# A decoder trunk: up- and query projections that begin with four units per input chunk instead of two, and a down unit whose weight halves are made in the last up pair

## The chip, the cores and the metric

The kernel runs on one core of a Trainium2 chip. The core has TensorE (PE, matrix products into PSUM), VectorE (DVE), ScalarE (ACT), GpSimd (POOL) and SyncE (SP, which issues the DMAs here). The metric is the time of one execution on the device in microseconds; lower is better. The engines run their own instruction lists in order and meet through semaphores.

## The reference

Two layers work on x (512 positions, 1024 features, float32). Each has a token mixer and a gated MLP, each inside a pre- and a post-norm, with a residual.

```python
for i in range(DEPTH):                       # DEPTH = 2
    hn = rmsnorm(x, norm_mix_pre[i])
    m = mamba2_mixer(hn, ...) if i % 2 == 0 else diff_attention(hn, ...)
    x = x + rmsnorm(m, norm_mix_post[i])
    hn = rmsnorm(x, norm_ffn_pre[i])
    f = conv_ffn(hn, ffn_w_up[i], ffn_conv_w[i], ffn_conv_b[i], ffn_w_down[i])
    x = x + rmsnorm(f, norm_ffn_post[i])
```

`conv_ffn` projects 1024 features to 2 x 2816, convolves causally with width 3, and projects silu(gate) * up back to 1024. `diff_attention` projects to q, k and v for 8 heads and subtracts one softmax from another.

## The kernel before, in words

Everything is kept transposed: 128 features on the partitions, 512 positions along the row. x is 8 chunks of 128x512.

*Units.* Each projection is a phase (MIX, SOUT, UP0, DN0, QKV, AOUT, UP1, DN1), and a phase is a row of units. A unit of an in-phase is one 128-column block of the weights, 128x1024, for one output tile of 128x512. To keep float32 accuracy each operand is split in two halves of the fast format: w = w_hi + w_lo, hn = hn_hi + hn_lo. `product` makes three matmuls for one chunk, (w_hi, hn_hi), (w_hi, hn_lo), (w_lo, hn_hi) (L354 to L356); a unit of 8 chunks is 24 matmuls. A down unit is half a contraction, 11 chunks, 33 matmuls.

*Weights.* SyncE loads unit j into `raw` (2 slots, `load_unit`, L310), once the low half of unit j-2 is made. `split_hi` (ScalarE, L317) copies it to w_hi, once unit j-2 has been multiplied, since w_hi and w_lo have two slots too. Then VectorE (`split_lo_dve`, L330), or GpSimd during the QKV phase (`split_lo`, L323), subtracts: w_lo = raw - w_hi. `ahead` lets a phase's loop make the halves of the next phase's first units.

*Banks.* A unit sums into one of two PSUM banks (`acc_of`); `wait_bank` holds TensorE until the tile two units back has been taken. b_x and b_y (two banks each) serve the state-space mixer, the start of SOUT and the attention scores.

*A boundary.* Between an out-phase and the next in-phase stand a post-norm, the residual and a pre-norm (`boundary_pe`, `boundary_act`, `boundary_dve`, `boundary_pool`). TensorE sums the squares over partitions (`sum_stat`, L449 and L453), ScalarE takes the root (L376), VectorE puts the inverse on a diagonal (L381), TensorE broadcasts it (`norm_bcast`, L409) into b_norm. Then, chunk by chunk: VectorE scales mbuf (L544), VectorE or GpSimd adds it to x (L560, L521), ScalarE makes hn_hi (L510) and the square (L425), VectorE makes hn_lo (L534), GpSimd adds up the squares (L441). TensorE multiplies each chunk by two units as it comes. The pre-norm's factor is not in hn: it is a factor of each position, so the projections start without it, and it is broadcast last and copied to r_pre (L516). Each output tile is multiplied by r_pre when VectorE takes it out of its bank (L706 in the MLPs, L1335 and L1338 for q, k and v). Boundary 1 leads from SOUT to UP0, 2 from DN0 to QKV, 3 from AOUT to UP1; 0 and 4 are the ends.

*MLP.* `ffn_dve` goes over 22 pairs (gate tile, up tile): take the gate tile, its convolution (L709, L715), take the up tile, its convolution, product with the Silu (L1150). In the middle of each convolution (`mid`) it makes the low half of a coming unit.

*Attention.* Round h projects q, k, v of head h (units 3h to 3h+2), while head h-1 is scored and head h-2 is finished. Round 0 has projections alone. TensorE writes scores to b_x and b_y; VectorE adds the bias (L1347) and takes the maximum (L1351), ScalarE the exponentials (L1278), VectorE combines the two softmaxes; TensorE transposes the weights of the four query blocks (t0 to t3, L1209) into b_cb, and ScalarE copies each out (L1286) before the next.

## Time and profile before

| | |
|---|---|
| median of 3 runs | 1544.0 us (1543.45 to 1544.49) |
| profiled execution: its own time, its span | 1545.04 us, 1542.9 us |
| busy, share of the span: TensorE | 1466.8 us, 95% |
| VectorE | 1019.0 us, 66% |
| ScalarE | 613.6 us, 40% |
| GpSimd | 212.2 us, 14% |
| mean granted TensorE clock | 0.980 |
| DMA | 142.04 MB, mean 92 GB/s |

The span runs from the first to the last instruction of the profiled execution. Busy time counts work and not waiting. The granted clock is the share of TensorE's full speed.

### The profile page before, as it was taken

To read this page: it belongs to the slowest core of one execution; us is meant where nothing else is said; L and a number is where in the kernel's file an instruction comes from. 1 tells how busy PE (TensorE), PEld (TensorE's weight loads), DVE (VectorE), ACT (ScalarE), POOL (GpSimd) and SP (SyncE) were. 2 spreads that over 40 slices of the span, in tenths; PEclk is the share of its full clock that TensorE was granted. 3 is DMA by queue.
4 is the path that set the end of the run, shared out by engine and by line. 5 is a ranking of instruction groups with operands and counts; after the bars stand their busy time and mean duration, and the time that the engine had idled before them with its cause. 6 is when DMAs were issued, how large, how long until landed. Compare 5 with 4: busy or idle time off the path is not lost.

```text
span 1542.9 us, 20707 instructions
## 1 busy us (share of the span) xinstructions
PE 1466.8 (95%) x6774; PEld 1161.7 (75%) x6774; DVE 1019.0 (66%) x1417; ACT 613.6 (40%) x953; POOL 212.2 (14%) x134
## 2 busy tenths in 40 slices
PE   6999999999997999999999799999888999999996
PEld 5778888888785888888888477776657888888885
DVE  6788888888328887778322657778258777775223
ACT  5655555556324222223222436556343222222221
POOL 3011101011213000000011432321140000000111
PEclk9999999999998999999999899999889999999998
DMA  4433333332220322223222121211112222223221
GB/s 148 154 123 123 135 121 110 136 122 82 83 94 31 106 90 89 93 95 111 94 93 83 36 88 55 68 54 55 48 62 72 92 95 95 95 95 113 94 93 55
DMA packets 36273, 142.04 MB, mean 92 GB/s; under 512 B 4048, under 2 KB 4176, under 8 KB 34192
## 3 DMA queue, kind: packets, MB, share of 16 engines
q1 hardware_dynamic: 36240, 141.62, 26.9%
q8 instruction: 18, 0.29, 0.1%
q14 instruction: 15, 0.12, 0.0%
HBM read 139.38 MB, written 2.23 MB: 92 GB/s over the span
## 4 chain that ended last, share of the span: by engine, by line
PE 74%; issue 10%; DVE 10%; POOL 3%; ACT 2%; DMA 1%; DVEq 0%; SPq 0%; POOLq 0%; ACTq 0%
PE bank L354 23%; PE bank L356 22%; PE bank L355 22%; POOL w_lo L323 3%; DVE hn_lo L534 2%; DVE w_lo L330 2%; DVE mbuf L544 1%; DMA raw<-w_mix 1%; DVE x L560 1%; DVE cv_s L715 1%; ACT w_hi L317 1%; PE b_y L731 1%; PE b_x L743 1%; PE b_y L734 1%; PE b_norm L453 0%
## 5 line engine op out<-in xcount | busy, mean ns | idle before, releaser
L354 PE MATMUL bank<-hn_hi,w_hi 128*128 128x512 f32 x1288 | 522.3, 406 | 43.1 <-DVE hn_lo L534 35.0
L355 PE MATMUL bank<-hn_lo,w_hi 128*128 128x512 f32 x1288 | 513.3, 399 | 0.0
L356 PE MATMUL bank<-hn_hi,w_lo 128*128 128x512 f32 x1288 | 513.1, 398 | 0.0
L317 ACT ACTIVATE w_hi<-raw 128x1024 fp32r<-128x1024 f32 (+1 forms) x217 | 239.7, 1104 | 499.9 <-PE bank L356 482.1
L330 DVE TENSOR_TENSOR w_lo<-raw,w_hi 128x1024 fp32r<-128x1024 f32 (+1 forms) x194 | 257.9, 1330 | 259.1 <-ACT w_hi L317 258.4
L354 PEld LDWEIGHTS bank<-hn_hi,w_hi 128*128 128x128 f32 x1288 | 244.7, 190 | 119.5 <-issue 30.0
L356 PEld LDWEIGHTS bank<-hn_hi,w_lo 128*128 128x128 f32 x1288 | 244.5, 190 | 59.6
L355 PEld LDWEIGHTS bank<-hn_lo,w_hi 128*128 128x128 f32 x1288 | 244.9, 190 | 55.6
L356 PE MATMUL bank<-h_hi,w_lo 128*128 128x512 f32 x352 | 139.2, 396 | 0.0
L354 PE MATMUL bank<-h_hi,w_hi 128*128 128x512 f32 x352 | 139.2, 396 | 0.0
L355 PE MATMUL bank<-h_lo,w_hi 128*128 128x512 f32 x352 | 139.2, 396 | 0.0
L441 POOL TENSOR_TENSOR ssq<-ssq,sq 128x512 f32<-128x512 f32 x48 | 85.2, 1775 | 226.9 <-ACT sq L425 225.9
L706 DVE TENSOR_TENSOR ug_f<-bank,r_pre 128x512 f32<-128x512 f32 x88 | 60.8, 691 | 54.8 <-PE bank L356 54.5
L439 POOL COPY ssq<-sq 128x512 f32<-128x512 f32 x8 | 9.6, 1199 | 595.0 <-ACT sq L425 595.0
L354 PEld LDWEIGHTS bank<-h_hi,w_hi 128*128 128x128 f32 x352 | 66.1, 188 | 16.1
L356 PEld LDWEIGHTS bank<-h_hi,w_lo 128*128 128x128 f32 x352 | 66.1, 188 | 16.0
L355 PEld LDWEIGHTS bank<-h_lo,w_hi 128*128 128x128 f32 x352 | 66.1, 188 | 15.9
L715 DVE SCALAR_TENSOR_TENSOR cv_s<-ug_s,par,cv_s 128x512 f32<-128x512 f32 x96 | 71.9, 749 | 7.6 <-DVE cv_s L715 1.1
L1112 ACT ACTIVATE sg<-cg 128x512 f32<-128x512 f32 x44 | 27.8, 633 | 119.6 <-DVE cg L715 119.6
L323 POOL TENSOR_TENSOR w_lo<-raw,w_hi 128x1024 fp32r<-128x1024 f32 x23 | 54.9, 2388 | 131.6 <-ACT w_hi L317 131.6
L715 DVE SCALAR_TENSOR_TENSOR cu<-ug_f,par,cu 128x512 f32<-128x512 f32 x88 | 65.9, 749 | 6.2 <-DVE cu L715 6.1
L715 DVE SCALAR_TENSOR_TENSOR cg<-ug_f,par,cg 128x512 f32<-128x512 f32 x88 | 65.9, 749 | 6.0 <-DVE cg L715 0.3
(202 smaller groups left out, 1675.0 us busy)
## 6 DMA issues: line engine op xcount, KB each, us to landing
raw<-w_up SPq DMA_DIRECT2D x88, 512.0 KB, 3.3
raw<-w_mix SPq DMA_DIRECT2D x49, 512.0 KB, 3.3
raw<-w_dn SPq DMA_DIRECT2D x32, 704.0 KB, 4.0
raw<-w_qkv SPq DMA_DIRECT2D x24, 512.0 KB, 3.2
acs_bc<-scratch SPq DMA_DIRECT2D x8, 1024.0 KB, 5.3
ecs_bc<-scratch SPq DMA_DIRECT2D x8, 1024.0 KB, 4.6
raw<-w_sout SPq DMA_DIRECT2D x16, 512.0 KB, 3.3
raw<-w_aout SPq DMA_DIRECT2D x8, 512.0 KB, 3.2
```

The lines of the kernel that those rows point to most:

```text
L317: nc.scalar.activation(w_hi[:, slot, 0:ph.width], raw[:, slot, 0:ph.width], ACT.Copy).then_inc(hi_made, 1)
L323: nc.gpsimd.tensor_tensor(w_lo[:, slot, 0:ph.width], raw[:, slot, 0:ph.width], w_hi[:, slot, 0:ph.width].bitcast(F32), ALU.subtract).then_ ...
L330: nc.vector.tensor_tensor(w_lo[:, slot, 0:ph.width], raw[:, slot, 0:ph.width], w_hi[:, slot, 0:ph.width].bitcast(F32), ALU.subtract).then_ ...
L354: nc.tensor.matmul(acc[:], wh, hi, start=first, stop=False)
L355: nc.tensor.matmul(acc[:], wh, lo, start=False, stop=False)
L356: return nc.tensor.matmul(acc[:], wl, hi, start=False, stop=last)
L441: nc.gpsimd.tensor_tensor(ssq[:], ssq[:], sq[:, rep % 2, :], ALU.add).then_inc(sq_added, 1)
L534: nc.vector.scalar_tensor_tensor(hn_lo[:, m, :], x[:, m, :], gain(*GAINS[b][1], m), hn_hi[:, m, :].bitcast(F32), ALU.mult, ALU.subtract).t ...
L544: ins = nc.vector.scalar_tensor_tensor(mbuf[:, m, :], mbuf[:, m, :], gain(*GAINS[b][0], m), b_norm[:], ALU.mult, ALU.mult)
L706: nc.vector.tensor_tensor(ug[:, taps - 1:taps - 1 + S], acc_of(ph, rep)[:], r_pre[:], ALU.mult).then_inc(evac["in"], 1)
L715: ins = nc.vector.scalar_tensor_tensor(dst, ug[:, t:t + S], col(wcol + t), dst, ALU.mult, ALU.add)
L1112: nc.scalar.activation(sg[:], cg[:], ACT.Silu).then_inc(gate_ready, 1)
```

## The change

Three in-phases, UP0, QKV and UP1 (`WIDE`), begin with four units per chunk (`wide_start`). Their units 0 and 1 sum in b_y, 2 and 3 in b_x. TensorE starts as soon as the first chunk of hn_hi is there: for chunk 0 it makes the eight products with the high half first and the four with hn_lo after them. Chunks 1 to 5 are taken by all four units; then each unit takes chunks 6 and 7 alone, in the order 2, 3, 0, 1, with the statistic sum behind the first and the broadcast of the pre-norm before the last. Units 0 and 1 have their halves in new buffers (fx in the MLPs, ax for QKV), so four units' halves are there at once; halves of units 0 to 2 are made at the end of the phase before, 3 and 4 in the boundary. At a boundary VectorE makes hn_lo of chunk 0 before it scales chunk 2.

From there on the up phases use four banks in turn (bank0, bank1 and the two of b_x), and ScalarE and VectorE make, in pair m, the halves of units 2m+4 and 2m+5, where it was 2m+2 and 2m+3 (pair 0 makes those of units 5 and 6, pair 1 those of unit 7). So the last pairs make the first three units of the down phase. In QKV, units 0 to 3 are multiplied in the boundary; round 1 has units 4 and 5 left. GpSimd makes low halves from unit 5 on.

The core of the diff (the rest hands the new arguments through; VectorE's pairs read like ScalarE's):

```diff
+            fx_hi, fx_lo = sb("fx_hi", [P, 2, KC * P], F32R, scope=ffn), sb("fx_lo", [P, 2, KC * P], F32R, scope=ffn)
...
+            ax_hi, ax_lo = sb("ax_hi", [P, 2, KC * P], F32R, scope=att), sb("ax_lo", [P, 2, KC * P], F32R, scope=att)
...
+        def halves_of(ph, j, first=False):
+
+            if first and ph in WIDE and j < 2:
+                hi, lo = (ax_hi, ax_lo) if ph is QKV else (fx_hi, fx_lo)
+                return hi[:, j, 0:ph.width], lo[:, j, 0:ph.width]
+            slot = slot_of(ph, j)
+            return w_hi[:, slot, 0:ph.width], w_lo[:, slot, 0:ph.width]
...
+        def first_acc(ph, j):
+
+            return (b_x if j >= 2 else b_y)[:, j % 2, :] if ph in WIDE else acc_of(ph, j)
+
+        def up_acc(ph, j, first=False):
+
+            if first:
+                return first_acc(ph, j)
+            return b_x[:, j % 2, :] if j % 4 >= 2 else acc_of(ph, j)
...
+            first = ph in WIDE and isinstance(j, int)
             act.wait_ge(raw_in[slot], 8 * U + (16 - 8 * slot))
-            if not (isinstance(j, int) and U < 2):
+            if first and j < 2:
+                act.wait_ge(unit_done, ph.U0 - 2)
+            elif first and j in (2, 3, 4, 5):
+                act.wait_ge(unit_done, U - 3)
+            elif not (isinstance(j, int) and U < 2):
                 act.wait_ge(unit_done, U - 1)
-            nc.scalar.activation(w_hi[:, slot, 0:ph.width], raw[:, slot, 0:ph.width],
+            nc.scalar.activation(halves_of(ph, rep, first and j < 2)[0], raw[:, slot, 0:ph.width],
...
+            pv = ph.prev
+            if ph in (DN0, DN1) and isinstance(j, int) and j < 2:
+                pe.wait_ge(evac["in"], pv.before["in"] + pv.chunks - 3 + j)
+            elif ph is QKV and isinstance(j, int) and j in (4, 5):
+                pe.wait_ge(evac["out"], pv.before["out"] + pv.chunks - 5 + j)
+            elif isinstance(j, int) and j < 2:
+                if pv is not None:
                     pe.wait_ge(evac[pv.kind], pv.before[pv.kind] + pv.chunks - 1 + j)
             else:
...
+        def wait_up_bank(pe, ph, j):
+
+            pv = ph.prev
+            if isinstance(j, int) and j in (4, 5):
+                pe.wait_ge(evac["out"], pv.before["out"] + pv.chunks - 5 + j)
+            else:
+                pe.wait_ge(evac["in"], ph.before["in"] + j - 3)
...
+            if nxt in WIDE:
+                wide_start(pe, b, nxt)
+                return
...
+        def wide_start(pe, b, nxt):
+
+            def chunk(j, c):
+                return product(first_acc(nxt, j), 0, c, hn_hi[:, c, :], hn_lo[:, c, :], c == 0, c == KC - 1,
+                               halves_of(nxt, j, True))
+
+            pe.wait_ge(hnhi_ready, KC * b + 1)
+            for j in range(4):
+                pe.wait_ge(lo_made, nxt.U0 + j + 1)
+                wh, wl = halves_of(nxt, j, True)
+                nc.tensor.matmul(first_acc(nxt, j), wh[:, 0:P], hn_hi[:, 0, :], start=True, stop=False)
+                nc.tensor.matmul(first_acc(nxt, j), wl[:, 0:P], hn_hi[:, 0, :], start=False, stop=False)
+            pe.wait_ge(hnlo_ready, KC * b + 1)
+            for j in range(4):
+                nc.tensor.matmul(first_acc(nxt, j), halves_of(nxt, j, True)[0][:, 0:P], hn_lo[:, 0, :],
+                                 start=False, stop=False)
+            for c in range(1, KC - 2):
+                pe.wait_ge(hnlo_ready, KC * b + c + 1)
+                for j in range(4):
+                    chunk(j, c)
+            for n, j in enumerate((2, 3, 0, 1)):
+                for c in (KC - 2, KC - 1):
+                    pe.wait_ge(hnlo_ready, KC * b + c + 1)
+                    last = chunk(j, c)
+                last.then_inc(unit_done, 1)
+                if n == 0:
+                    wait_x_scaled(pe, b)
+                    sum_stat(pe, f"pre{b}")
+                elif n == 2:
+                    norm_bcast(pe, norm_no[f"pre{b}"])
+
...
-                    split_hi(act, nxt, 1, 1)
+                    split_hi(act, nxt, 3, 3)
...
-            norm_root(act, norm_no[f"pre{b}"])
-            ahead(split_hi, act, nxt, 2)
+            if b:
+                split_hi(act, nxt, 4, 4)
+                norm_root(act, norm_no[f"pre{b}"])
...
-                    split_lo_dve(dve, nxt, 1)
+                    split_lo_dve(dve, nxt, 3)
...
-                if b and m and m + 1 < KC:
+                if b and 1 < m and m + 1 < KC:
...
+                if b and m == 1:
+                    scale(2)
...
+                if b:
+                    split_lo_dve(dve, nxt, 4)
...
-            ahead(split, eng, ph, 4 * i + 2, 2)
+            if not (ph in (DN0, DN1) and isinstance(i, int) and i == 0):
+                ahead(split, eng, ph, 4 * i + 2, 2)
...
+            if last:
+                ahead(split, eng, ph, 4 * i + 5, 5)
+                ahead(split, eng, ph, 4 * i + 6, 6)
...
+            if last:
+                ahead(split, eng, ph, 2 * i + 3, 3)
+                ahead(split, eng, ph, 2 * i + 4, 4)
...
-                split_lo_dve(dve, nxt, 0)
+                for j in range(3):
+                    split_lo_dve(dve, nxt, j)
...
+            dve.wait_ge(unit_done, ph.U0 + j + (3 if first and j < 2 else 1))
...
-            with pe.Fori(1, FC) as m:
-                in_unit(pe, up, 2 * m, 0)
-                in_unit(pe, up, 2 * m + 1, 1)
+            in_unit(pe, up, 4, 4)
+            in_unit(pe, up, 5, 5)
+            in_unit(pe, up, 6, 6)
+            in_unit(pe, up, 7, 7)
+            with pe.Fori(2, FC // 2) as i:
+                for r in range(4):
+                    in_unit(pe, up, 4 * i + r, r)
...
+            pair(0, 5, 5, 6)
+            pair(1, 6, None, 7)
+            with act.Fori(1, FC // 2 - 1) as i:
+                pair(2 * i, 0, 4 * i + 4, 4 * i + 5)
+                pair(2 * i + 1, 2, 4 * i + 6, 4 * i + 7)
+            pair(FC - 2, 44, 2 * FC, 2 * FC + 1)
+            pair(FC - 1, 45, None, 46)
...
+            pair(0, 0, 5, 6, True)
+            pair(1, 2, None, 7, True)
+            with dve.Fori(1, FC // 2 - 1) as i, ch.loop(i, 1, FC // 2 - 2, 4 * (FFN_T - 1)):
+                pair(2 * i, 0, 4 * i + 4, 4 * i + 5)
+                pair(2 * i + 1, 2, 4 * i + 6, 4 * i + 7)
+            pair(FC - 2, 0, 2 * FC, 2 * FC + 1)
+            pair(FC - 1, 2, None, 46)
...
+            started = isinstance(h, int) and h == 0
+            starting = isinstance(h, int) and h == 1
+            if proj and not (started or starting):
                 in_unit(pe, QKV, 3 * h, rep)
+            if starting:
+                in_unit(pe, QKV, 3 * h + 1, rep + 1)
...
+                pe.wait_ge(evac["in"], QKV.before["in"] + 3 * h + (1 if starting else 0))
...
-            if proj:
+            if proj and not (isinstance(h, int) and h == 0):
...
+            out_phase_dve(dve, DN0, 2, QKV, first=3)
```

The order of instructions shows it at three places. First, TensorE at boundary 1, from the broadcast of the post-norm (L409) on. Before, it reads:

```order
L409 MATMUL b_norm<-diag,ones 128x512 [waits diag_ready]
L354 MATMUL bank1<-hn_hi,w_hi 128x512 [waits evac_out,lo_made,hnlo_ready]
L355 MATMUL bank1<-hn_lo,w_hi 128x512
L356 MATMUL bank1<-hn_hi,w_lo 128x512
L354 MATMUL bank0<-hn_hi,w_hi 128x512
L355 MATMUL bank0<-hn_lo,w_hi 128x512
L356 MATMUL bank0<-hn_hi,w_lo 128x512
L354 MATMUL bank1<-hn_hi,w_hi 128x512 [waits hnlo_ready]
```

After it reads, behind that broadcast (b_y holds units 0 and 1, b_x units 2 and 3; fx_hi, fx_lo are the new buffers; line numbers are those of the changed kernel):

```order
L554 MATMUL b_y<-hn_hi,fx_hi 128x512 [waits lo_made,hnhi_ready]
L555 MATMUL b_y<-hn_hi,fx_lo 128x512
L554 MATMUL b_y<-hn_hi,fx_hi 128x512 [waits lo_made]
L555 MATMUL b_y<-hn_hi,fx_lo 128x512
L554 MATMUL b_x<-hn_hi,w_hi 128x512 [waits lo_made]
L555 MATMUL b_x<-hn_hi,w_lo 128x512
L554 MATMUL b_x<-hn_hi,w_hi 128x512 [waits lo_made]
L555 MATMUL b_x<-hn_hi,w_lo 128x512
L558 MATMUL b_y<-hn_lo,fx_hi 128x512 [waits hnlo_ready]
L558 MATMUL b_y<-hn_lo,fx_hi 128x512
L558 MATMUL b_x<-hn_lo,w_hi 128x512 x2
L395 MATMUL b_y<-hn_hi,fx_hi 128x512 [waits hnlo_ready]
```

The first matmul waited for hn_lo and waits for hn_hi now, and eight matmuls with hn_hi stand ahead of the first that needs hn_lo. At the end of the same boundary, from the last chunk of unit 2 on, the changed kernel has:

```order
L395 MATMUL b_x<-hn_hi,w_hi 128x512 [waits hnlo_ready]
L396 MATMUL b_x<-hn_lo,w_hi 128x512
L397 MATMUL b_x<-hn_hi,w_lo 128x512
L495 MATMUL b_norm<-mean_col,ssq 128x1 [waits sq_added,x_new]
L495 MATMUL b_norm<-mean_col,ssq 128x1 x3
L499 MATMUL b_norm<-mean_col,sq 128x1 [waits sq_ready]
L499 MATMUL b_norm<-mean_col,sq 128x1 x3
L395 MATMUL b_x<-hn_hi,w_hi 128x512 [waits hnlo_ready]
L396 MATMUL b_x<-hn_lo,w_hi 128x512
L397 MATMUL b_x<-hn_hi,w_lo 128x512
```

The statistic sum stood ahead of the last chunk of both units; it stands now behind unit 2, with units 3, 0 and 1 after it.

Second, TensorE in attention round 1: from the scores of head 0 to the transposes t0 and t1 (L1209; L1322 in the changed kernel). Before (the rows left out are the matmuls of units 4 and 5):

```order
L1199 MATMUL b_x<-kT,qT 128x128 [waits evac_in]
L1199 MATMUL b_x<-kT,qT 128x128
L1199 MATMUL b_y<-kT,qT 128x256 x2
L354 MATMUL bank1<-hn_hi,w_hi 128x512 [waits evac_in,lo_made]
...
L1237 MATMUL b_cb<-ident,vT 128x128 x4
L1199 MATMUL b_x<-kT,qT 128x384 [waits s_taken]
L1199 MATMUL b_x<-kT,qT 128x384
L1199 MATMUL b_y<-kT,qT 128x512 [waits s_taken]
L1199 MATMUL b_y<-kT,qT 128x512
L354 MATMUL bank0<-hn_hi,w_hi 128x512 [waits evac_in,lo_made]
...
L1209 MATMUL b_cb<-ident,at 128x128 [waits a_ready,tr_copied] x2
```

After (the rows left out are the matmuls of unit 5):

```order
L1312 MATMUL b_x<-kT,qT 128x128 [waits evac_in]
L1312 MATMUL b_x<-kT,qT 128x128
L1312 MATMUL b_y<-kT,qT 128x256 x2
L1354 MATMUL b_cb<-ident,vT 128x128 x4
L1312 MATMUL b_x<-kT,qT 128x384 [waits s_taken]
L1312 MATMUL b_x<-kT,qT 128x384
L1312 MATMUL b_y<-kT,qT 128x512 [waits s_taken]
L1312 MATMUL b_y<-kT,qT 128x512
L395 MATMUL bank0<-hn_hi,w_hi 128x512 [waits evac_out,lo_made]
...
L1322 MATMUL b_cb<-ident,at 128x128 [waits a_ready,tr_copied] x2
```

Unit 4, which stood between the first scores and the transposes of v, has moved ahead of the scores, so that one unit is left between the first scores and t0.

Third, ScalarE at the end of SOUT: the halves of the last SOUT unit and of UP0's first ones, and the square and copy of output chunks 6 and 7, to the root of the post-norm. Before:

```order
L317 ACTIVATE w_hi<-raw 128x1024 [waits unit_done,raw_in0]
L317 ACTIVATE w_hi<-raw 128x1024 [waits unit_done,raw_in1]
L425 ACTIVATE sq<-bank1 128x512 [waits sq_added,unit_done]
L640 ACTIVATE mbuf<-bank1 128x512
L425 ACTIVATE sq<-bank0 128x512 [waits sq_added,unit_done]
L640 ACTIVATE mbuf<-bank0 128x512
L376 ACTIVATE root<-b_norm,eps 128x4 [waits stat_ready]
```

After:

```order
L344 ACTIVATE w_hi<-raw 128x1024 [waits unit_done,raw_in0]
L344 ACTIVATE fx_hi<-raw 128x1024 [waits unit_done,raw_in1]
L344 ACTIVATE fx_hi<-raw 128x1024 [waits unit_done,raw_in0]
L344 ACTIVATE w_hi<-raw 128x1024 [waits unit_done,raw_in1]
L471 ACTIVATE sq<-bank1 128x512 [waits sq_added,unit_done]
L726 ACTIVATE mbuf<-bank1 128x512
L471 ACTIVATE sq<-bank0 128x512 [waits sq_added,unit_done]
L726 ACTIVATE mbuf<-bank0 128x512
L422 ACTIVATE root<-b_norm,eps 128x4 [waits stat_ready]
```

One split for UP0 stood ahead of the square of chunk 6; three stand there now. The last of them, unit 2's, waits for the same SOUT unit as the square does.

## Rows read from the trace of the kernel before

**Rows 1.** Waits of TensorE over the whole span: us in total, times, longest us.

```profile
PE bank L354 <- DVE hn_lo L534: 35.0, 13, 10.7
```

**Rows 2.** Busy time by stretch: length, busy us (instructions) by engine, granted clock, DMA share, GB/s.

```profile
472.20:477.00 4.80, 4.76 (x11) 3.33 (x12) 4.80 (x6) 2.64 (x6) 4.40 (x4) 0.50 0.02 3
500.00:520.00 20.00, 20.00 (x87) 16.12 (x86) 17.17 (x24) 6.55 (x8) 0.00 (x0) 1.00 0.31 105
862.90:866.30 3.40, 3.36 (x7) 2.30 (x8) 3.40 (x4) 1.86 (x4) 3.00 (x3) 0.51 0.00 0
1078.00:1082.00 4.00, 1.86 (x8) 1.19 (x8) 3.82 (x11) 3.25 (x11) 0.00 (x0) 0.91 0.00 2
1082.00:1086.00 4.00, 4.00 (x16) 3.13 (x15) 0.98 (x2) 1.09 (x2) 0.00 (x0) 0.67 0.00 0
```

**Rows 3.** Timeline of TensorE at boundary 1: start us, us, engine, instruction [idle before <-releaser].

```profile
472.24 0.77 PE L354 MATMUL bank<-hn_hi,w_hi 128*128 128x512 f32 x1 [4.21 <-DVE hn_lo L534]
...
489.10 0.95 PE L449 MATMUL b_norm<-mean_col,ssq 128*128 128x1 f32 x8
...
490.80 0.48 PE L354 MATMUL bank<-hn_hi,w_hi 128*128 128x512 f32 x1
...
492.28 1.07 PE L409 MATMUL b_norm<-diag,ones 128*128 128x512 f32 x2
494.96 0.50 PE L354 MATMUL bank<-hn_hi,w_hi 128*128 128x512 f32 x1 [1.61 <-DVE ug_f L706]
...
506.27 0.40 PE L354 MATMUL bank<-hn_hi,w_hi 128*128 128x512 f32 x1
```

**Rows 4.** Timeline of ScalarE and of VectorE at boundary 1.

```profile
469.58 0.72 ACT L510 ACTIVATE hn_hi<-x,par 128x512 fp32r<-128x512 f32 x1 [3.25 <-DVE x L560]
...
470.78 1.32 DVE L534 SCALAR_TENSOR_TENSOR hn_lo<-x,par,hn_hi 128x512 fp32r<-128x512 f32 x1
...
483.44 1.75 DVE L534 SCALAR_TENSOR_TENSOR hn_lo<-x,par,hn_hi 128x512 fp32r<-128x512 f32 x1
...
494.22 0.69 DVE L706 TENSOR_TENSOR ug_f<-bank,r_pre 128x512 f32<-128x512 f32 x1
```

**Rows 5.** Timeline at boundaries 2 and 3, ScalarE and TensorE.

```profile
860.28 0.72 ACT L510 ACTIVATE hn_hi<-x,par 128x512 fp32r<-128x512 f32 x1 [3.67 <-DVE x L560]
...
896.99 0.49 PE L1199 MATMUL b_x<-kT,qT 64*128 64x128 f32 x4
...
1143.21 0.72 ACT L510 ACTIVATE hn_hi<-x,par 128x512 fp32r<-128x512 f32 x1 [3.67 <-DVE x L560]
...
1179.89 0.40 PE L354 MATMUL bank<-hn_hi,w_hi 128*128 128x512 f32 x1
```

**Rows 6.** Timeline of attention round 1: VectorE, ScalarE, TensorE.

```profile
898.08 0.48 DVE L1347 SCALAR_TENSOR_TENSOR sc<-dist,slopes,b_x 128x256 f32<-128x256 f32 x1
...
903.75 0.69 DVE L1338 TENSOR_TENSOR kT<-bank,r_pre 128x512 f32<-128x512 f32 x1 [1.01 <-PE bank L356]
905.05 1.02 DVE L1347 SCALAR_TENSOR_TENSOR sc<-dist,slopes,b_x 128x768 f32<-128x768 f32 x1 [0.60 <-PE b_x L1199]
...
911.79 0.28 ACT L1286 ACTIVATE aT<-b_cb 128x128 f32<-128x128 f32 x1 [0.73 <-PE b_cb L1209]
...
912.42 0.50 PE L354 MATMUL bank<-hn_hi,w_hi 128*128 128x512 f32 x1
```

**Rows 7.** Timeline at the end of SOUT and in the first up pair; DMA issues.

```profile
452.26 1.06 ACT L317 ACTIVATE w_hi<-raw 128x1024 fp32r<-128x1024 f32 x1 [4.54 <-PE bank L356]
...
458.95 1.23 DVE L330 TENSOR_TENSOR w_lo<-raw,w_hi 128x1024 fp32r<-128x1024 f32 x1 [4.37 <-ACT w_hi L317]
...
459.55 1.79 POOL L441 TENSOR_TENSOR ssq<-ssq,sq 128x512 f32<-128x512 f32 x1 [15.01 <-ACT sq L425]
...
501.42 0.69 DVE L1150 TENSOR_TENSOR hb<-sg,cu 128x512 f32<-128x512 f32 x1
...
raw<-w_up SPq DMA_DIRECT2D x88, 512.0 KB, 3.3
```

112 lines of the change are left out of this document (58 added, 54 removed).

## The prediction

> **What bounds the kernel now.** I read the waits of TensorE first, then the busy time by stage, then the rows of one boundary one by one. The longest wait of TensorE is for the low halves hn_lo of the normalised input [rows 1]. Inside the projections there is nothing to gain: in 500 to 520 us TensorE is busy for 20.00 of 20.00 us, with VectorE busy for 17.17 [rows 2]. So the loss lies at the boundaries. At the one from the state-space mixer to the first gated MLP, ScalarE has the first chunk of hn_hi at 469.58 + 0.72 = 470.30, VectorE starts the low half at 470.78 [rows 4], and TensorE takes its first projection matmul only at 472.24, after 4.21 us of waiting [rows 3]. VectorE and GpSimd then deliver a chunk about every 2.6 us (chunk 0 at 470.78 + 1.32 = 472.10, chunk 5 at 483.44 + 1.75 = 485.19 [rows 4]), while two units use six matmuls of a chunk. One unit of 24 matmuls takes half of 506.27 - 494.96 = 11.31 us, so a slot is 0.236 us and six are 1.4 us [rows 3]: TensorE idles between chunks. The third unit starts at 494.96, 1.61 us late, since its bank is emptied only after the inverse root has been broadcast and copied [rows 3]. The reader is to see one figure: from the first hn_hi (470.30) until four units are done (506.27) there are 36.0 us for 22.6 us of projection matmuls.
>
> **The change, part by part.** *Removed at a boundary.* TensorE now starts with the high halves alone, and each chunk feeds twelve matmuls, 2.8 us, more than the 2.6 us that a chunk takes to come. So TensorE should be the bound from the first matmul. With chunk 0 begun at 470.4 and the first matmuls slow (below), chunk 5 is taken up at 470.4 + 60 x 0.236 + 2.2 = 486.8, 1.6 us after its hn_lo is there. That VectorE now makes lo(0) before scale(2), with a short wait for hn_hi, moves the later chunks by 0.2 to 0.3 us, within that margin.
> *Boundary 1 (UP0).* Start 470.4; 96 slots, 22.6 us; both statistic sums 490.80 - 489.10 = 1.7 us; the broadcast 1.1 us [rows 3]. Low clock: in 472.20 to 477.00 the granted clock was 0.50, the 1.2 GHz level, and 11 matmuls were issued in 4.80 us instead of 20.4, a loss of 2.2 us; at boundary 2 it was 3.40 us with 7 instead of 14.4, a loss of 1.7 us [rows 2]. TensorE starts as cold as before, so I charge 2.2 here. End 470.4 + 22.6 + 1.7 + 1.1 + 2.2 = 498.0, against 506.27 [rows 3]: **8.3 us**.
> *Boundary 3 (UP1).* hn_hi is there at 1143.21 + 0.72; with 0.1 for the handover and 1.7 for the clock the end is 1144.0 + 22.6 + 2.8 + 1.7 = 1171.1, and before the fifth unit began at 1179.89 [rows 5]: **8.8 us**, of which I take off 0.1 for ScalarE's queue (below): **8.7 us**.
> *Boundary 2 (QKV), the matmuls.* 860.28 + 0.72 + 0.1 = 861.1, plus 22.6 + 2.8 + 1.7, is 888.2. Before, four units were done as the scores began, 896.99 [rows 5]: 8.8 us.
> *Boundary 2, what comes behind it.* Two of the units that used to lie between the attention steps of round 1 are now spent. Unit 4 runs first (to 893.85), then the scores, the transposes of v, the other scores, unit 5, and the transposes t0 and t1. t1 waits for ScalarE's copy of t0, which is queued behind all four exponentials, and these behind VectorE. Before, from the first bias (898.08) to the first matmul of unit 6 (912.42) there were 14.34 us, with three waits for TensorE inside: 1.01, 0.60 and 0.73 [rows 6]. Without them the chain is 12.0 us. It now starts 0.1 + 0.55 us (the first scores) after 893.85, and releases unit 6 at 906.5. TensorE's own work would be through at about 893.85 + (912.42 - 896.99) - 5.7 = 903.6, the round without unit 4. So a new stall of about 3 us appears in front of t1, and of the 8.8 us 912.42 - 906.5 = 5.9 stay.
> *The clock in that stall.* No row has such a gap between such matmuls, so bounds: nothing, if the clock stays at 2.4 GHz, and 1.7 us if it falls as at a boundary. The nearest rows are 1078 to 1086: TensorE busy for 1.86 of 4.00 us at 0.91, then for 4.00 of 4.00 at 0.67, a third of 4 us lost, 1.3 us [rows 2]. I take 1.3: **4.6 us** for this boundary.
> The Trainium skill (TensorE: Matmul & The Clock Gate, HAM oscillation) holds that a TensorE that waits some microseconds between bursts is throttled again and pays the cold start each time. By it the stall costs the full cold start and the sum is 0.4 us smaller than with my value; the trace agrees as far as 1078 to 1086 goes.
> *Halves made earlier.* Units 0 and 1 go to buffers of their own (fx, ax), so ScalarE makes three high halves ahead of the last two evacuations of the phase, where it made one. Who waits: the square of chunk 6, GpSimd's add of it (1.79 us), and the post-norm sum. At boundary 1 the last half of SOUT is split from 452.26; a split is 1.06 us on ScalarE and 1.23 on VectorE, and a load lands 3.3 us after its issue [rows 7]. Unit 2's load is issued when unit 0's low half is made (455.8), lands at 459.1, its high half ends at 460.2, the square at 460.8, GpSimd's add at 462.6. The sum starts when TensorE ends, about 463.2: hidden with 0.6 us to spare. At boundary 3 two evacuations stand between as well, and the margin is about nothing (the 0.1 above). At boundary 2 a unit is 33 matmuls, and the cover is larger. If loads were 1 us later, it would cost 0.4 and 1 us.
> *VectorE one pair behind in the up projections.* It leaves the boundary with four units to empty. Pair 0 took 494.22 to 502.1, 7.9 us with one split inside [rows 4, 7]. Now it starts near 497.3 with two, the second bound to the end of unit 4 (503.6): its low half is made at 506.2, the pair ends at 508.4, and unit 2's bank is free at 509.1. TensorE wants it for unit 6 at 498.0 + 11.3 = 509.3. The margin is 0.2 us, so I charge nothing; a delay there would be paid one for one, at two places. Later VectorE has 2.8 us of slack in 20 [rows 2] and catches up; weights for unit 2m+4 are ready some 2.4 us after its slot is free, and wanted 5.6 us after. From unit 6 on four banks cover the lag.
> *The third down unit.* Its halves wait for down unit 0 (33 slots, 7.8 us) and are wanted 15.5 us after the up phase ends. VectorE, a pair behind, makes them after some 12 us. Nothing gained, nothing lost. The splits that move from GpSimd to VectorE in QKV (two) fall where VectorE waits anyway.
> *Sum.* 8.3 + 8.7 + 4.6 = 21.6 us. Against the profiled execution (span 1542.9, 1545.04 us by its own time) that is a span of about 1521.3; the profiled execution is 1.0 us above the median of 1544.0, and I take the difference off the median: **1522.4 us**.
>
> **The rivals.**
> *The full gain.* The attention chain is no bound, since the real waits are shorter than I linked them, and QKV gives its 8.8 us too: 8.3 + 8.7 + 8.8 = 25.8, or 1518. Against it: the fixed order of ScalarE's queue. 0.12.
> *Late covers.* The loads come later, or the ramp of the up projections misses its 0.2 us by one or two: 1 us at three post-norm chains, 1.5 us at each of two ramps and 1.7 instead of 1.3 for the clock give 21.6 - 6.4 = 15.2, or 1529. For it: two margins under 1 us. 0.19.
> *Slower: the up loop becomes bound by VectorE.* The whole body now runs a pair late, with ScalarE's order split, copy of hb, Silu. If VectorE's cycle for a pair exceeded 11.3 us, TensorE would wait in each of 20 pairs in two layers. It decides from 21.6 / 40 = 0.54 us a pair; with 1 us a pair the time is 1544.0 - 21.6 + 40 = 1562. Against it: VectorE's load, 17.17 of 20 us [rows 2], is not changed by the order, and the banks are now four. 0.04.
> *The change does not do what it says.* Chunks come too slowly to feed four units, so that TensorE waits for VectorE as before. Then the end hangs on chunk 5: 485.19, plus 36 slots (8.5 us) for the last three chunks, plus 2.8 us, is 496.5. That is under 506.27 too, and chunk 5 would have to come almost 10 us later than in the trace to bring this gain to nothing. For a time within 0.2% several of the above would have to meet: 0.02.
>
> **How the numbers follow.** The forecast (gain of 18 to 24.5) has 0.63, the full gain 0.12, late covers 0.19, slower 0.04, no change 0.02. 0.2% is 3.1 us, about what a measurement of this kernel tells from no change. The range reaches to both neighbours: 1517 takes in the full gain with the clock cost at nothing, 1529 the late covers; together they leave out about 0.15. Faster: 0.94, same 0.02, slower 0.04.
>
> **What would show it.** After: no wait of over 1 us for hn_lo at boundaries 1 to 3; 96 projection matmuls without a gap from some 2 us earlier than before, to about 27 to 28 us later; no wait for ug_f at unit 4; a new wait of about 3 us for ScalarE's aT in front of the first attention round's t1, perhaps with a lower clock behind it; TensorE fully busy in the up loops. Wrong would be: a wait at units 6 or 7 of the up projections (bank or w_lo), or a post-norm sum that waits for GpSimd.

## The result, and the profile after

| | before | after |
|---|---|---|
| median (range, runs) | 1543.72 us (1543.45 to 1544.49, 4) | 1526.76 us (1526.15 to 1527.99, 4) |
| profiled execution: its own time, its span | 1545.04, 1542.9 | 1526.15, 1524.4 |
| TensorE busy | 1466.8 us, 95% | 1460.8 us, 96% |
| mean granted clock | 0.980 | 0.983 |

The ratio is 0.989, 95% interval 0.9878 to 0.9902: 17.0 us faster by the medians, 18.5 by the spans. The forecast was 1522.4 us; the time is inside its range and 4.4 us above the point.

TensorE's waits in the changed kernel (line, releaser: us in total, times, longest), against the 35.0 us of [rows 1]:

```profile
PE bank L395 <- DVE hn_lo L615: 11.1, 1, 11.1
PE b_y L554 <- ACT hn_hi L587: 7.0, 3, 2.3
...
PE b_cb L1322 <- ACT aT L1403: 4.7, 4, 2.7
...
PE b_y L395 <- DVE hn_lo L615: 2.6, 3, 1.0
...
PE b_norm L495 <- POOL ssq L487: 0.9, 2, 0.6
```

The 11.1 us are the head of the program (10.7 of the 35.0 before), which the change leaves alone. At the three boundaries the wait for hn_lo has shrunk from 24.3 to 2.6 us, all of it for the second chunk (chunk 1). TensorE now waits 7.0 us for hn_hi of the first chunk, a part of what it waited for hn_lo before. Two small waits are new: for GpSimd's sum of squares, and in the attention round for ScalarE's copy.

The timeline of TensorE at boundary 1, which answers to [rows 3]:

```profile
469.72 0.80 PE L554 MATMUL b_y<-hn_hi,fx_hi 128*128 128x512 f32 x1 [2.32 <-ACT hn_hi L587]
...
475.90 0.50 PE L395 MATMUL b_y<-hn_hi,fx_hi 128*128 128x512 f32 x1 [0.80 <-DVE hn_lo L615]
...
493.11 0.47 PE L395 MATMUL b_x<-hn_hi,w_hi 128*128 128x512 f32 x1
...
498.22 0.40 PE L395 MATMUL bank<-hn_hi,w_hi 128*128 128x512 f32 x1
```

The first matmul comes at 469.72 (472.24 before) and the fifth unit at 498.22 (506.27). Between them there is one gap, 0.80 us in front of chunk 1. From its first matmul to the fifth unit each of the three wide starts takes 28.5 us.

Busy time by stretch, the columns as in [rows 2]:

```profile
469.70:474.90 5.20, 5.18 (x12) 3.84 (x12) 5.20 (x5) 2.43 (x5) 4.80 (x4) 0.51 0.10 41
474.90:498.20 23.30, 22.50 (x103) 18.05 (x103) 15.45 (x19) 9.06 (x16) 9.87 (x7) 1.00 0.06 23
495.00:520.00 25.00, 25.00 (x107) 19.75 (x107) 19.19 (x28) 8.43 (x10) 0.00 (x0) 1.00 0.24 85
```

Chunk 0's twelve matmuls run at a granted clock of 0.51, the 1.2 GHz level, as the first matmuls did before. From 474.90 on the clock is full. Across the old pinch at units 4 to 6 TensorE is busy for 25.00 of 25.00 us.

Where the time went, from TensorE's rows in both traces (us; a stretch goes from the start of the first to the start of the second; "sum" is the statistic sum of the post-norm):

| stretch | before | after | gain | forecast |
|---|---|---|---|---|
| boundary 1: sum to DN0's first matmul | 267.08 | 259.16 | 7.9 | 8.3 |
| of it unit 4 to DN0 | 224.0 | 224.0 | 0 | 0 |
| boundary 2: sum to AOUT's first matmul | 212.24 | 207.82 | 4.4 | 4.6 |
| boundary 3: sum to DN1's first matmul | 267.49 | 260.11 | 7.4 | 8.7 |
| SOUT's first matmul to the sum | 98.22 | 98.74 | -0.5 | 0 |
| AOUT's first matmul to the sum | 70.69 | 71.43 | -0.7 | in the 8.7 |
| DN0 and DN1, first matmul to the sum | 123.2 each | 123.2 each | 0 | 0 |

They sum to 18.4; the spans differ by 18.5 (what lies ahead of SOUT is 0.65 us shorter, what lies behind the last sum 0.6 longer). The medians differ by less because the profiled execution of before lies 1.3 us above its median and that of after 0.6 below.

Of the 18.4 us, 1.5 are not the change's. The broadcast of the post-norm at boundaries 1 and 2 took 1.12 and 1.13 us in this execution, at a granted clock of 1.00, and 1.65 and 2.07 in that of before, at 0.64 and 0.50. The first matmul came sooner by that. Other executions have the long broadcast in the same place: 1.93 and 2.07 us in square_first, which has nothing changed behind the sum there.

### The profile page after: what moved, and what is told of

It is laid out like the page before. It is cut to its first block, busy times and chain, and to the rows that moved or that the text cites. A ratio compares the mean times of both kernels' runs of the same rounds, so it can differ in the third digit from the quotient of the medians.

```text
span 1524.4 us, 20441 instructions
## 1 busy us (share of the span) xinstructions
PE 1460.8 (96%) x6774; PEld 1161.9 (76%) x6774; DVE 1021.5 (67%) x1419; ACT 612.2 (40%) x953; POOL 206.5 (14%) x132
## 3 DMA queue, kind: packets, MB, share of 16 engines
q1 hardware_dynamic: 36240, 141.62, 27.2%
## 4 chain that ended last, share of the span: by engine, by line
PE 74%; issue 10%; DVE 8%; POOL 3%; ACT 3%; DMA 2%; DVEq 0%; SPq 0%; POOLq 0%; ACTq 0%
PE bank L395 17%; PE bank L396 16%; PE bank L397 16%; PE b_x L395 6%; PE b_x L396 6%; PE b_x L397 6%; POOL w_lo L350 3%; DVE w_lo L358 2%; DMA raw<-w_mix 1%; DVE cv_s L812 1%; ACT w_hi L344 1%; PE b_y L828 1%; DVE mbuf L625 1%; DVE hn_lo L615 1%; PE b_y L395 1%
## 5 line engine op out<-in xcount | busy, mean ns | idle before, releaser
L395 PE MATMUL bank<-hn_hi,w_hi 128*128 128x512 f32 x872 | 351.8, 403 | 16.8 <-DVE hn_lo L615 11.1
L396 PE MATMUL bank<-hn_lo,w_hi 128*128 128x512 f32 x872 | 345.6, 396 | 0.0
L397 PE MATMUL bank<-hn_hi,w_lo 128*128 128x512 f32 x872 | 345.6, 396 | 0.0
L395 PEld LDWEIGHTS bank<-hn_hi,w_hi 128*128 128x128 f32 x872 | 164.7, 189 | 60.2 <-issue 13.0
L397 PEld LDWEIGHTS bank<-hn_hi,w_lo 128*128 128x128 f32 x872 | 164.4, 188 | 39.6
L396 PEld LDWEIGHTS bank<-hn_lo,w_hi 128*128 128x128 f32 x872 | 164.7, 189 | 37.6
L395 PE MATMUL b_x<-hn_hi,w_hi 128*128 128x512 f32 x362 | 143.4, 396 | 0.0
L397 PE MATMUL b_x<-hn_hi,w_lo 128*128 128x512 f32 x362 | 143.2, 395 | 0.0
L396 PE MATMUL b_x<-hn_lo,w_hi 128*128 128x512 f32 x362 | 143.1, 395 | 0.0
L395 PEld LDWEIGHTS b_x<-hn_hi,w_hi 128*128 128x128 f32 x362 | 68.0, 188 | 16.5 <-issue 0.2
```

Source lines behind the costliest of these rows:

```text
L395: nc.tensor.matmul(acc[:], wh, hi, start=first, stop=False)
L396: nc.tensor.matmul(acc[:], wh, lo, start=False, stop=False)
L397: return nc.tensor.matmul(acc[:], wl, hi, start=False, stop=last)
```

## The experiments

Each kernel is the changed one with the edit shown, unless it says otherwise. The time of before, measured beside them, was 1543.72 for the first four, 1543.18 for the next four and 1544.06 for the last two (medians of 9, 9 and 15 runs). It moves by up to 0.9 us from one group to the next, so a difference of 1 us between kernels of different groups says little.

| | median (range) | ratio to before [95%] |
|---|---|---|
| changed kernel | 1526.76 (1526.15 to 1527.99) | 0.989 [0.9878, 0.9902] |
| scale_first | 1522.64 (1521.46 to 1523.74) | 0.9859 [0.9844, 0.9874] |
| square_first | 1525.04 (1523.63 to 1527.09) | 0.9878 [0.9863, 0.9894] |
| copy_first | 1523.56 (1521.90 to 1524.59) | 0.9865 [0.985, 0.9881] |
| all_three | 1521.03 (1515.62 to 1523.13) | 0.9846 [0.9827, 0.9865] |
| qkv_two | 1529.85 (1528.92 to 1531.21) | 0.9917 [0.9903, 0.993] |
| low_half_first | 1526.85 (1525.34 to 1527.13) | 0.9892 [0.9877, 0.9907] |
| all_three_low_half_first | 1522.53 (1521.61 to 1525.44) | 0.9871 [0.9856, 0.9886] |
| kept_warm | 1515.55 (1514.86 to 1517.28) | 0.9822 [0.9809, 0.9835] |
| changed_kept_warm | 1530.44 (1527.13 to 1531.97) | 0.9914 [0.9901, 0.9928] |
| before_kept_warm | 1544.56 (1539.49 to 1545.35) | 0.9999 [0.9989, 1.0009] |

**scale_first: VectorE scales chunk 2 ahead of hn_lo of chunk 0 again, as before the change.**

```diff
-                if b and 1 < m and m + 1 < KC:
+                if b and m and m + 1 < KC:
...
-                if b and m == 1:
-                    scale(2)
```

> The changed kernel, with one part undone: VectorE scales chunk 2 before it makes hn_lo of chunk 0 again, as before the change. Theory A (the swap is the mis-sized term): in the changed kernel hn_lo of chunk 0 began earlier but took 1.78 us beside GpSimd's add instead of 1.32, and hn_lo of chunk 1 was ready 8.41 us after the first scale instead of 6.98, so TensorE waited 0.8, 0.8 and 1.0 us for it. Undone, these three waits go and the time falls by about 2.5 us, to 1524.3. Theory B (the chunks come too slowly in any order, TensorE as fast as it is would wait at a later chunk instead): the wait moves to chunk 3 or 5 and the time stays within 0.7 us of 1526.8.

4.1 us faster by the medians, more than expected. In its waits the 2.6 us for hn_lo are gone, and the wide starts take 27.6, 27.6 and 27.1 us instead of 28.5, which is 3.3 us in all. In this trace the broadcasts at boundaries 1 and 2 were the long ones (2.08 us), so the fifth unit comes no sooner after the sum there than in the changed kernel's trace (35.2 us in both). The cause stands in the changed kernel's rows of VectorE and GpSimd at boundary 1:

```profile
469.65 1.28 POOL L602 TENSOR_TENSOR x<-x,mbuf 128x512 f32<-128x512 f32 x1 [6.73 <-DVE mbuf L625]
469.70 1.78 DVE L615 SCALAR_TENSOR_TENSOR hn_lo<-x,par,hn_hi 128x512 fp32r<-128x512 f32 x1
...
472.06 0.74 DVE L625 SCALAR_TENSOR_TENSOR mbuf<-mbuf,par,b_norm 128x512 f32<-128x512 f32 x1
...
472.72 1.45 DVE L641 TENSOR_TENSOR x<-x,mbuf 128x512 f32<-128x512 f32 x1
...
474.09 1.76 DVE L615 SCALAR_TENSOR_TENSOR hn_lo<-x,par,hn_hi 128x512 fp32r<-128x512 f32 x1
```

and in those of scale_first, VectorE alone:

```profile
469.97 1.40 DVE L625 SCALAR_TENSOR_TENSOR mbuf<-mbuf,par,b_norm 128x512 f32<-128x512 f32 x2
471.28 1.34 DVE L615 SCALAR_TENSOR_TENSOR hn_lo<-x,par,hn_hi 128x512 fp32r<-128x512 f32 x1
...
473.20 0.68 DVE L641 TENSOR_TENSOR x<-x,mbuf 128x512 f32<-128x512 f32 x1
473.81 1.77 DVE L615 SCALAR_TENSOR_TENSOR hn_lo<-x,par,hn_hi 128x512 fp32r<-128x512 f32 x1
```

In the changed order the low half of chunk 0 begins as GpSimd begins its add, and takes 1.78 us instead of 1.34; the add of the next x also falls beside an operation of GpSimd and takes 1.45 instead of 0.68. From the first scaling (467.44) to the end of the second hn_lo (475.85) there are 8.4 us, against 7.0 before (468.07 to 473.28 + 1.77 = 475.05). The forecast had counted only the order, 0.2 to 0.3 us, with durations taken over from a trace in which those operations had other neighbours.

**square_first: the halves of the next phase's unit 2 are made behind the square of output chunk 6.** The same move stands in the other out-phase loop.

```diff
             if last:
                 ahead(split, eng, ph, 4 * i + 5, 5)
-                ahead(split, eng, ph, 4 * i + 6, 6)
             chunk(2 * i, 0, 4 * i + 3)
             if last:
+                ahead(split, eng, ph, 4 * i + 6, 6)
```

> The changed kernel, with the last two output chunks' work on ScalarE put ahead of the third weight split: square and copy of chunk 6 come before unit 2's high half at the end of SOUT, DN0 and AOUT. Theory A (the splits ahead of the square delay the post-norm sum): TensorE's waits for GpSimd's last add (0.3 and 0.6 us) go, the sums of squares begin 0.3 to 0.5 us sooner at boundaries 1 and 3 and the time falls by about 1.0 us, to 1525.7. Theory B (the sum is bound by the last chunk's square anyway): the waits go but the roots come no sooner, and the time stays at 1526.8 within 0.3 us.

1.7 us faster by the medians, with ranges that overlap; the traces tell it apart better. The changed kernel, ScalarE, GpSimd and TensorE ahead of boundary 1:

```profile
459.45 1.06 ACT L344 ACTIVATE w_hi<-raw 128x1024 fp32r<-128x1024 f32 x1 [1.00 <-DMA raw<-w_up]
...
460.42 0.58 ACT L471 ACTIVATE sq<-bank 128x512 f32<-128x512 f32 x1
...
461.14 1.78 POOL L487 TENSOR_TENSOR ssq<-ssq,sq 128x512 f32<-128x512 f32 x1 [17.24 <-ACT sq L471]
...
463.06 0.35 PE L495 MATMUL b_norm<-mean_col,ssq 128*128 128x1 f32 x2 [0.32 <-POOL ssq L487]
```

ScalarE waits 1.00 us for the load of unit 2, its square is late by that, and GpSimd ends at 462.92, just behind TensorE's last product. In square_first GpSimd starts that add 3.5 us ahead of the sum (457.42 and 460.93) where it was 1.9, the wait is gone, and the two stages are back at 98.24 and 70.70 us: 1.2 us. This wait was named ahead as what would be wrong.

**copy_first: in round 1 ScalarE copies t0 out ahead of the fourth exponential.**

```diff
-                probs(3)
-                copy_back(0, "t0", h - 1)
+                if isinstance(h, int) and h == 1:
+                    copy_back(0, "t0", h - 1)
+                    probs(3)
+                else:
+                    probs(3)
+                    copy_back(0, "t0", h - 1)
```

> The changed kernel, with ScalarE's copy of the transposed block t0 put between the third and the fourth exponentials in attention round 1 alone. Theory A (TensorE's wait of 2.72 us in front of t1 comes from ScalarE's order, and the low clock of the next seven matmuls from that wait): t1 follows t0 by about 0.4 us, the granted clock stays at full speed, and the time falls by 2.4 + 1.4 = 3.8 us, to 1523.0. Theory B (the chain behind it is bound by VectorE: combine 3, the maxima): unit 6 begins sooner, but TensorE waits later in round 2 for t2, t3 or the scores, and the time falls by less than 1.5 us. In between: the wait goes and the clock falls anyway, 1524.4.

3.2 us faster. The stall and its clock in the changed kernel, the windows first:

```profile
895.00:898.20 3.20, 0.57 (x4) 0.17 (x2) 3.09 (x7) 2.07 (x8) 0.00 (x0) 0.98 0.43 160
898.30:902.00 3.70, 3.70 (x11) 3.04 (x12) 1.55 (x5) 1.15 (x2) 2.74 (x1) 0.57 0.01 2
```

```profile
898.29 0.69 PE L1322 MATMUL b_cb<-ident,at 128*128 128x128 f32 x2 [2.72 <-ACT aT L1403]
898.63 0.78 PE L395 MATMUL bank<-hn_hi,w_hi 128*128 128x512 f32 x1
```

TensorE waits 2.72 us in front of t1 (2.9 had been forecast), and then the clock is 0.57 for 3.7 us, while TensorE is busy throughout. At 1.00 the eleven instructions would have taken about 3.7 x 0.57 = 2.1 us, so the clock costs up to 1.6; seven projection matmuls at 0.43 instead of 0.23 are 1.4. In copy_first ScalarE has the copy done at 896.46 + 0.28, TensorE waits 0.37 us, and the clock stays up:

```profile
896.79 0.44 PE L1322 MATMUL b_cb<-ident,at 128*128 128x128 f32 x2 [0.37 <-ACT aT L1403]
```

```profile
896.00:902.00 6.00, 5.63 (x26) 4.27 (x25) 5.82 (x11) 3.27 (x9) 2.06 (x1) 1.00 0.23 81
```

Boundary 2 to AOUT takes 204.12 us instead of 207.82: 3.7 us, so both the stall and its clock come back. The Trainium skill (TensorE: Matmul & The Clock Gate, HAM oscillation) holds that a TensorE that waits some microseconds between bursts starts each burst cold; the 0.57 here agrees. Two waits of 3.1 and 3.2 us in changed_kept_warm, below, were not followed by a low clock.

**all_three: the three edits together.**

> The changed kernel with all three edits: scale of chunk 2 first, square of chunk 6 first, copy of t0 between the exponentials. If the three costs are independent they add up: 2.5 + 1.0 + 3.8 = 7.3 us, 1519.5, which is below both kernels. If they only move waits to the next place (theory B of each), at least 1524.

5.7 us faster by the medians, with runs from 1515.6 to 1523.1. The single gains add up to 9.0; medians of kernels that scatter by 2 to 7 us don't add up to the last us, and the forecast of the sum was 1.5 us too hopeful. From the sum to the fifth unit it takes 33.83, 34.96 and 35.03 us (35.16, 35.17 and 36.12 in the changed kernel). At boundary 2 the broadcast was long here (2.07 us) and short in the changed kernel's trace (1.13); with like broadcasts the gain is 1.1 to 1.3 us at each boundary.

**qkv_two: QKV begins with two units and keeps its old rounds; UP0 and UP1 keep four.** The conditions on `first`, `starting` and the splits follow the same table.

```diff
-        WIDE = (UP0, QKV, UP1)
+        WIDE = (UP0, UP1)
```

> The changed kernel, with one part undone: QKV begins with two units per chunk as before, with its waits, splits and order on all engines; UP0 and UP1 keep four units. Theory A (each boundary gives its own share, and boundary 2 gave 4.4 us by the traces, 8.2 less a stall of 2.7 and a low clock of 1.4): the time rises by 4.4 us to 1531.2, the wait in front of t1 goes back to 0.4 us. Theory B (boundary 2 gave nothing, the stall took it all): 1526.8 within 1 us.

3.1 us slower, 1.3 less than expected. From the sum of boundary 2 to AOUT it takes 210.79 us, between the changed kernel's 207.82 and before's 212.24. Before's wait for hn_lo is back at this boundary and the stall at t1 is gone. Of the 1.4 us that stay against before, 0.94 are an earlier start, 8.53 us after the sum against 9.47: the broadcast took 1.13 us here and 2.07 there. Nothing shows where the other 0.5 come from. The sign is clear, and QKV gives about as much as forecast.

**low_half_first: TensorE waits for hn_lo of chunk 0 before its first matmul.** The order of matmuls stays.

```diff
-            pe.wait_ge(hnhi_ready, KC * b + 1)
+            pe.wait_ge(hnlo_ready, KC * b + 1)
...
-            pe.wait_ge(hnlo_ready, KC * b + 1)
```

> The changed kernel, but TensorE waits for hn_lo of chunk 0 before its first projection matmul at boundaries 1 to 3, as before the change. Theory A (the early start is worth only what the later wait for chunk 1 leaves): the start moves 1.8 us later, the wait of 0.8 to 1.0 us for chunk 1 goes, and the time rises by about 0.9 us a boundary, 2.7 us in all, to 1529.5. Theory B (the early start is worth all of its 1.8 us): 5.4 us, 1532.2.

Both theories missed: 0.1 us, nothing. At boundaries 2 and 3 TensorE starts 8.44 and 9.40 us after the sum instead of 6.64 and 7.61, 1.8 us later, yet the fifth unit begins after 35.16 and 36.10 us, against 35.17 and 36.12. (At boundary 1 it is 36.09 against 35.16; the broadcast took 2.08 us there and 1.12 in the changed kernel's trace.) The wait for chunk 1 has gone instead. In the changed kernel the end of the wide start therefore hangs on chunk 1 and not on the first matmul: 475.90 to 498.22 is the rest of the work without a gap, and what TensorE does before 475.90 is free.

**all_three_low_half_first: the same with the three orders put back.**

> The kernel with all three edits, but TensorE waits for hn_lo of chunk 0 before its first matmul at boundaries 1 to 3. Here chunk 1 is not waited for, so theory A says that the whole 1.8 us of the early start are lost at each of three boundaries, 5.4 us over the kernel with all three edits (about 1520 to 1525.5). Theory B (the clock would have risen later anyway, so the cold matmuls are only shifted): under 2 us.

1.5 us slower than all_three by the medians, 3.4 by the means (1523.0 against 1519.6), less than the 5.4 of theory A. From sum to fifth unit: 35.11, 35.12 and 36.26, so 1.3, 0.2 and 1.2 us slower than all_three. The 0.2 hides 0.9 us of broadcast (1.13 us here, 2.07 there); with like broadcasts it is 1.1 to 1.3 us at each boundary, 3.6 in all. Once chunk 1 is in time, an earlier start is worth that much and not the full 1.8 us: begun later, eight or nine matmuls run at 1.2 GHz (0.43 us each) where ten to twelve did, so the wide starts take 26.7, 26.7 and 26.9 us instead of 27.2, 27.4 and 27.4.

**kept_warm: all_three with useless matmuls, five ahead of and eight behind the post-norm's broadcast.** They pass the time in which TensorE waits; nothing reads their result.

```diff
+            def warm(n):
+                for _ in range(n):
+                    nc.tensor.matmul(b_cb[:], ones_r[:], diag_hi[:].rearrange("p b t -> p (b t)"),
+                                     start=True, stop=True)
...
                 sum_stat(pe, f"post{b}")
+                if nxt is not None:
+                    warm(5)
                 norm_bcast(pe, norm_no[f"post{b}"])
+                if nxt is not None:
+                    warm(8)
```

> The kernel with all three edits, and TensorE makes 5 matmuls of no use (ones_r by diag_hi into b_cb, which nothing reads then) between the post-norm's sum and its broadcast and 8 behind the broadcast, at boundaries 1 to 3. Theory A (TensorE starts cold because it idles in the norm; the cold start costs 1.7 to 2.2 us a boundary plus up to 0.9 us in the broadcast): kept busy it starts at the full clock, and the time falls by 5 to 7 us to about 1514. Theory B (with a warm TensorE the chunks of VectorE become the bound, so that what the clock gives is lost in waits for hn_lo): it falls by less than 2.5 us. Theory C (the filling matmuls delay the broadcast or the start): it rises.

5.5 us faster than all_three by the medians, 3.9 by the means, 3.7 by the ratios to before (whose intervals meet), 27.6 faster than before, and within 2.4 us from run to run where all_three's runs lie within 7.5. The windows of boundary 1:

```profile
462.86:466.10 3.24, 3.21 (x23) 2.64 (x21) 0.93 (x3) 2.29 (x4) 0.00 (x0) 1.00 0.55 174
470.40:475.00 4.60, 3.06 (x14) 2.12 (x12) 4.60 (x6) 2.79 (x5) 4.20 (x4) 1.00 0.00 0
475.00:497.00 22.00, 21.99 (x101) 17.82 (x102) 15.47 (x18) 8.38 (x14) 10.94 (x7) 1.00 0.08 25
```

No matmul of the wide start is slow. But in the second window TensorE is busy for 3.06 of 4.60 us: the wait for chunk 1 is back (5.0 us at three places), and the chunks are the bound again. So theory B holds for the wide starts: they take 26.9, 27.1 and 27.1 us, only 0.3 us less than in all_three. From the sum to the fifth unit the trace shows 34.49, 33.73 and 33.71 us against 33.83, 34.96 and 35.03, 1.9 us less in all, most of it the broadcast (1.86, 1.13 and 1.12 us against 1.12, 2.07 and 2.07), and the spans differ by 1.3. The rest of the 5.5 is that three of all_three's five runs lie at 1521 to 1523 us, 4 to 6 above its profiled one, and none of kept_warm's does. No trace shows where those three lost it, and the two kernels were measured in different groups.

**changed_kept_warm: the same useless matmuls in the changed kernel, its three orders left as they are.**

> The changed kernel, none of the three orders put back, with useless matmuls added (five ahead of and eight behind the broadcast of the post-norm at boundaries 1 to 3). They pass through TensorE's wait, so that it is not idle before the projections; they compute nothing that is used. Theory A (cold matmuls and late chunks hide each other): while the first matmuls are slow, a late chunk 1 costs little; with full speed the chunks are the bound, and the order scale(2), lo(0) costs the same 2.6 us and more. So the filler gives less than the 5.5 us it gave over the kernel with the three orders put back: 2 to 4 us, to about 1523 to 1525, and the wait for hn_lo grows from 2.6 to over 5 us. Theory B (the clock is a cost of its own): 5 to 6 us as there, to about 1521.

Neither theory: 3.7 us slower by the medians. TensorE at boundary 1, with the windows behind:

```profile
469.27 0.40 PE L563 MATMUL b_y<-hn_hi,fx_hi 128*128 128x512 f32 x1
...
475.20 0.70 PE L395 MATMUL b_y<-hn_hi,fx_hi 128*128 128x512 f32 x1 [2.97 <-DVE hn_lo L624]
```

```profile
469.27:471.80 2.53, 2.53 (x12) 2.06 (x11) 2.53 (x3) 1.46 (x3) 2.13 (x3) 1.00 0.00 0
471.80:474.30 2.50, 0.44 (x2) 0.00 (x0) 2.50 (x3) 0.79 (x2) 2.50 (x2) 1.00 0.00 0
474.30:478.60 4.30, 3.40 (x8) 2.72 (x9) 4.30 (x6) 1.62 (x4) 3.93 (x4) 0.62 0.00 0
```

Chunk 0 is done at full clock by 472.2, and then TensorE waits 2.97 us for chunk 1, with the low clock behind that wait, so that this wide start takes 29.8 us. At boundaries 2 and 3 no matmul is slow, the waits are 3.2 and 3.1 us, and the wide starts take 28.5 us, exactly what they take in the changed kernel with all twelve matmuls of chunk 0 slow. So theory A's reason holds (cold matmuls and the late chunk hide each other), but a gain was expected where there is none: in the changed kernel only the time of chunk 1 counts. Of the 3.7 us the trace shows about 1.3, at boundary 1; it is of the fastest of the five runs (1527.13). Whether the others lost more in the same way is not shown. Theory C of kept_warm is a rival for a part of it: at boundary 3 the first five useless matmuls ran slow themselves (2.21 us instead of 1.41), and the projections began 7.99 us after the sum instead of 7.61.

**before_kept_warm: the same in the kernel before.**

> The kernel before with the same useless matmuls at boundaries 1 to 3. There TensorE waits for hn_lo between the chunks (35.0 us in all), since two units use up a chunk faster than VectorE and GpSimd deliver it. Theory A: the cold start was free before, hidden in the wait for chunks, and only the changed kernel made it a cost; the time stays within 1 us of 1543.7, and the wait for hn_lo grows by what the matmuls save, some 5 us. Theory B: the cold start costs as much before as after, and the time falls by 3 us or more.

Theory A: 0.5 us above before, no difference. TensorE starts 8.53 us after the sum instead of 9.05 to 9.48 and runs the first chunk at full clock at boundaries 1 and 2, but from the sum to the third unit the three boundaries take 31.24, 31.18 and 31.25 us against 31.77, 32.16 and 32.19.

```profile
470.87 0.47 PE L354 MATMUL bank<-hn_hi,w_hi 128*128 128x512 f32 x1 [2.37 <-DVE hn_lo L543]
...
473.73 0.50 PE L354 MATMUL bank<-hn_hi,w_hi 128*128 128x512 f32 x1 [1.23 <-DVE hn_lo L543]
```

TensorE waits 1.23 us for the second chunk at once. The 0.5 to 1.0 us left at each boundary are the start that came earlier with a short broadcast (1.12 or 1.13 us at all three); of what the full clock gave to the first matmuls nothing is left, the chunks took it up. The 2.4 us of the three boundaries hardly show in the span, 1542.4 against 1542.9, because AOUT took 1.8 us longer in this execution (its clock is told in the last section).

## Why the prediction was nearly right, point by point

- **The bound and the mechanism: right.** The waits for chunks and for the third unit's bank are gone, the first matmul comes 1.9 to 2.8 us sooner after the sum, and the whole gain lies at the three boundaries. Of the earlier start 1.8 to 1.9 us are the change's, the rest at boundaries 1 and 2 is the broadcast's clock.
- **"Each chunk feeds twelve matmuls, 2.8 us, more than the 2.6 us that a chunk takes to come": right from chunk 1 on**; chunk 1 itself comes too late.
- **"That VectorE now makes lo(0) before scale(2) ... moves the later chunks by 0.2 to 0.3 us, within that margin": the step that failed.** Chunk 1 came 1.4 us later after the first scaling, and TensorE waited 0.8 to 1.0 us for it at each boundary. The wide starts took 28.5 us each, where the terms had 27.6, 27.1 and 27.1; at boundaries 1 and 2 a start 0.5 and 1.0 us earlier than forecast gave part of that back. That was luck: the forecast took the starts from a trace with long broadcasts, and this execution had short ones. Undoing the order gave 4.1 us by the medians, 3.3 in the wide starts.
- **The low clock at the start, 2.2 and 1.7 us: right in size, off in its use.** In scale_first, where nothing waits for chunk 1, the wide starts are 2.2, 2.2 and 1.7 us longer than their 25.4 us of work. But in the changed kernel the end did not hang on them: low_half_first and changed_kept_warm show that the time before chunk 1 is free. With the orders put back full clock shortened the wide starts by 0.3 us each, since chunk 1 became the bound again (kept_warm).
- **"Hidden with 0.6 us to spare", and at boundary 3 "about nothing" (0.1 charged): mis-sized.** The load of unit 2 kept ScalarE for 1.00 us at boundary 1 and 1.32 at boundary 3, GpSimd's sum came 0.32 and 0.59 us after TensorE was ready, and the stages grew by 0.5 and 0.7; square_first takes both back.
- **Boundary 2: right behind the wide start, near in the sum by luck.** 2.9 us of stall forecast, 2.72 measured; 1.3 us of clock forecast, about 1.4 measured; 4.6 and 4.4 us in all. The wide start itself was 1.4 us longer than forecast, and the short broadcast gave 1.0 of it back.
- **The ramp at unit 6, the up loops, the third down unit: right.** The stage from unit 4 to DN0 takes 224.0 us in both traces, DN0 123.20 in both; the margin of 0.2 us held. TensorE's waits for w_lo grew from 4.3 to 6.8 us, but none lies in an up phase; the growth is in the first mixer, before 115 us, which the change leaves alone.
- **The rivals.** The full gain fell with the stall at t1. Of the late covers, only those of the sums came, in part. No slower loop, and no wait for ug_f.
- The point was 4.4 us low: 1.9 of it at boundaries 1 to 3 (0.4, 0.2 and 1.3), 1.2 in the late sums, and the rest is how the two profiled executions lie to their medians. Without the short broadcasts the boundaries alone would have been 3.4 low.

## What to carry to other kernels

When a change reorders operations of an engine that works beside another, take their durations for the new neighbours and not from their old place; the first two operations of a pipeline set its end. Work out which single event the end hangs on, and count a cost ahead of it only where it moves that event: here slow matmuls were free while chunk 1 was late. A fix at the bound can turn neighbouring edits from worthless to useful: the early start gave nothing in the changed kernel (0.1 us) and 1.1 to 1.3 us a boundary once chunk 1 was in time. So test such edits together and not only one by one. And before two traces are compared, compare the short stretches whose clock differs from one execution to the next.
